# Four unused tensors that move the stationary matmul buffers by some bytes within a partition

## What is computed

```python
def first_block(x, p, ...):
    h = x
    for i in range(2):                      # i = 0: gated linear attention; i = 1: differential attention
        h = h + mixer(rms_norm(h, norm_mix[i]))
        h = h + swiglu(rms_norm(h, norm_ffn[i]), ffn_w_in[i], ffn_w_out[i])   # D_FF = 2816
        gate = sigmoid(rms_norm(h, ple_norm[i]) @ ple_w_gate[i])
        h = h + gate * (p[i] @ ple_w_proj[i])                                # p[i]: 256 wide
    return h

def second_block(x, ...):
    h = x
    for i in range(2):                      # i = 0: short convolution; i = 1: block attention, 16 heads
        h = h + mixer_2(rms_norm_2(h, norm_g[i]))
    return h
```

## Time and profile before

| | |
|---|---|
| median of the runs (lowest, highest) | 986.59 us (985.86, 987.36) |
| span of the profiled execution, first to last instruction | 983.4 us |
| median less span | 3.2 us |
| TensorE busy | 956.9 us, 97% |
| TensorE weight loads | 773.6 us, 79% |
| VectorE / ScalarE / GpSimd busy | 609.7 / 510.3 / 74.0 us |
| TensorE in the chain that ended last | 87% |
| line 1304 in that chain | 76% |
| granted clock of TensorE, mean | 0.996 |

### The profile page before, as it was taken

One profiled execution on the slowest core, in us unless ns is written; L12 is line 12 of the kernel. 1 busy time (PEld: TensorE's weight loads), 2 busy tenths in 40 slices (PEclk: granted clock), 3 DMA queues, 4 the chain that ended last, 5 costly groups with the idle time before them and its releaser, 6 DMA issues.

```text
span 983.4 us, 13238 instructions
## 1 busy us (share of the span) xinstructions
PE 956.9 (97%) x4532; PEld 773.6 (79%) x4532; DVE 609.7 (62%) x895; ACT 510.3 (52%) x821; POOL 74.0 (8%) x82
## 2 busy tenths in 40 slices
PE   7999999999999999878999999999999999999998
PEld 6786688888888888656788888888878888878777
DVE  5774556665655477886575565644577776565552
ACT  6854355434444466567563444443754444666470
POOL 0000000000000005531100000000000000302000
PEclk9999999999999999999999999999999999999999
DMA  7643246556555456332366555544555554542411
GB/s 280 215 154 118 96 144 200 189 173 193 190 193 176 146 166 209 119 105 74 98 214 191 186 178 189 175 172 161 203 181 186 189 195 146 192 152 96 145 60 43
DMA packets 45629, 159.73 MB, mean 162 GB/s; under 512 B 5099, under 2 KB 6891, under 8 KB 45580
## 3 DMA queue, kind: packets, MB, share of 16 engines
q1 hardware_dynamic: 45580, 159.06, 49.1%
HBM read 157.99 MB, written 1.05 MB: 162 GB/s over the span
## 4 chain that ended last, share of the span: by engine, by line
PE 87%; DVE 7%; ACT 2%; POOL 2%; issue 1%; DMA 1%; POOLq 0%; SPq 0%; ACTq 0%; DVEq 0%
PE bank L1304 76%; PE bank L1326 2%; DVE wlo L767 1%; PE bank L1528 1%; PE bank L1456 1%; DVE df_stat L1087 1%; PE bank L1479 1%; PE bank L1628 1%; PE bank L1710 1%; PE bank L1709 1%; ACT df_p L629 1%; PE bank L1732 1%; DVE df_m L1060 1%; DMA h<-x_dram 1%; PE bank L1718 0%
## 5 line engine op out<-in xcount | busy, mean ns | idle before, releaser
L767 DVE TENSOR_TENSOR wlo<-raw,whi 128x1024 fp32r<-128x1024 f32 (+1 forms) x297 | 350.6, 1217 | 66.3 <-ACT whi L418 66.1
L418 ACT ACTIVATE whi<-raw 128x1024 fp32r<-128x1024 f32 (+1 forms) x297 | 306.0, 1057 | 143.4 <-PE bank L1304 115.0
L1304 PE MATMUL bank<-whi,x_hi 128*128 128x512 f32 x592 | 236.9, 400 | 0.4 <-DVE x_lo L783 0.4
L1304 PE MATMUL bank<-whi,x_lo 128*128 128x512 f32 x592 | 231.2, 390 | 0.0
L1304 PE MATMUL bank<-wlo,x_hi 128*128 128x512 f32 x592 | 230.7, 390 | 0.0
L1304 PE MATMUL bank<-whi,y_hi 128*128 128x512 f32 x400 | 160.5, 401 | 0.8 <-DVE y_lo L1185 0.4
L1304 PE MATMUL bank<-whi,y_lo 128*128 128x512 f32 x400 | 157.0, 393 | 0.0
L1304 PE MATMUL bank<-wlo,y_hi 128*128 128x512 f32 x400 | 156.8, 392 | 0.0
L1304 PEld LDWEIGHTS bank<-whi,x_hi 128*128 128x128 f32 x592 | 111.2, 188 | 29.9 <-issue 7.1
L1304 PEld LDWEIGHTS bank<-whi,x_lo 128*128 128x128 f32 x592 | 111.1, 188 | 23.9
L1304 PEld LDWEIGHTS bank<-wlo,x_hi 128*128 128x128 f32 x592 | 111.3, 188 | 21.2
(11 more groups left out here) (208 smaller groups left out, 933.3 us busy)
## 6 DMA issues: line engine op xcount, KB each, us to landing
raw<-stream_dram SPq DMA_DIRECT2D x296, 512.0 KB, 4.2
h<-x_dram SPq DMA_DIRECT2D x4, 256.0 KB, 3.4
out<-h SPq DMA_DIRECT2D x4, 256.0 KB, 2.0
consts<-consts_dram SPq DMA_DIRECT2D x1, 576.0 KB, 8.9
p_tok<-p_dram SPq DMA_DIRECT2D x1, 512.0 KB, 9.4
rows<-rows_dram SPq DMA_DIRECT2D x1, 256.0 KB, 9.6
gla_wgate<-wgate_dram SPq DMA_DIRECT2D x1, 132.0 KB
raw<-stream_dram SPq DMA_DIRECT2D x1, 128.0 KB, 2.6
```

The lines of the kernel that those rows point to most:

```text
L418: A(whi[:, u % RING, 0:w], raw[:, u % RAW, 0:w], ACT.Copy).then_inc(sem("w_hi"), 1)
L767: V.tensor_tensor(wlo[:, u % RING, 0:w], raw[:, u % RAW, 0:w], whi[:, u % RING, 0:w].bitcast(F32), ALU.subtract).then_inc(sem("w_lo"), 1)
L1304: last = T.matmul(bank[pair + t][:, :], lhs[a][:, kt, t * P:(t + 1) * P], w[:, u % RING, kk * NW:(kk + 1) * NW], start=part != 1 and k == ...
```

## The change

Four tensors that no instruction reads or writes are declared between the others. That is the whole change.

```diff
         h = sb("h", [P, TT, D])
+        sb("before_x", [P, 16])
         X = (sb("x_hi", [P, KT, SEQ], F32R), sb("x_lo", [P, KT, SEQ], F32R))
+        sb("before_y", [P, 48])
         Y = (sb("y_hi", [P, KT, SEQ], F32R), sb("y_lo", [P, KT, SEQ], F32R))
+        sb("before_p", [P, 72])
         PT = (sb("p_hi", [P, 2, SEQ], F32R), sb("p_lo", [P, 2, SEQ], F32R))
         p_tok = sb("p_tok", [P, 2, TT, PLE])
         cols = sb("cols", [P, N_COLS])
@@
         neg_half = sb("neg_half", [P, 16])
         rstd_q = sb("rstd_q", [P, TT])
+        sb("before_phases", [P, 48])
         ident = consts[:, K_ID:K_ID + P]
```

## The result

The changed kernel took 992.28 us in the median of 13 runs (988.66 to 994.71), the kernel before 986.59 (981.37 to 991.46, 13 runs). The ratio is 1.0046, with a 95% interval of 1.003 to 1.0063. The change makes the kernel slower, by some 4.5 to 7 us. The forecast was 983.7 us, faster. The measured time lies in the stated range, which was drawn to hold every case of a loss too, but the change has the other sign.

The account below looks back on a forecast made before the run. TensorE, busy 97% of the span, was taken as the bound. Span 983.4 - 3.2 (`mid`) + 0.3 (`PT`) + 0 = 980.5 us, plus 3.2 gives 983.7 us; range of 8 in 10: 978 to 1002 us.

Parts of the forecast that it names:

- the term of `X`, 128 to 192: 1776 matmuls with `X` stationary: taken as 0, with 10.1 us more as the bound if they took `mid`'s pace.
- 416 is slow since it is no multiple of 64: Reading of the two phases seen: 416 is 6 x 64 + 32 and slow; 192 and 384, multiples of 64, cost 0.
- The argument that 64 bytes of the stream last about one step: 64 of the moving 2048 bytes take 7.1 ns, the step is 6.4 ns; phase 416 touches 9 pieces, 128 covers 8.
- `mid` gained 3.2 us: 528 matmuls with `mid`, phase 416 to 128: forecast 3.2 us less, FFN-out's piece of 96 at 21.8 us from 22.40.
- `Y` at 384: 1200 matmuls with `Y`, phase 128 to 384: taken as 0, with 6.8 us more as the bound.
- `PT`: 48 matmuls with `PT`, phase 128 to 160: forecast 0.3 us more, at `mid`'s slow pace.
- Transposes and plain matmuls: 480 transposes and some 470 mixer matmuls: taken as 0, bounds 3.1 us more and some 3.0 us less.
- the lost lock: Rival: pace needs both streams at matching phases; `X` alone 993.8 us, `Y` alone 990.5; chance 0.26, 0.14 for one buffer.
- the slow restart behind transposes at phase 128: Trace row cited for a rival: behind transposes ten steps of 232 ns each, then eight of 226 ns, at phase 128 too.
- Its full form, both buffers: Rival case where `X` and `Y` both lose the pace and `mid` gains: 14.0 us more, 1000.6 us, chance 0.12.
- The 3.2 us that the prediction put around the span: Step from span to time: the median stands 3.2 us above the profiled span, so 980.5 us becomes 983.7 us.
- The rule of the Trainium skill: TensorE's operands use independent ports and lines of 16 bytes: no phase should matter, time stays 986.6 us.

Follow-up runs that it names:

- e9: The kernel before with `X` alone moved, to phase 192; `Y` and `PT` stay at 128, `mid` at 416: 995.61 us, ratio 1.0098.
- e3: The kernel before with the moving rings and `X` at phase 192, `Y` at 384, `PT` at 448, `mid` at 256: 990.08 us in one run.
- e8: The kernel before with everything from `raw` on 64 bytes up and `mid` at 192, so rings and all four stationary buffers at phase 192: 983.84 us, ratio 0.9979.
- e10: The kernel before with `X`, `Y`, `PT` and `mid` at phase 192 and the moving rings left at 128: 1001.71 us, ratio 1.0154.
- e11: The kernel before with the moving rings alone at phase 192; `h` and all four stationary buffers stand at 128: 985.39 us in one run.
- e2: The kernel before with one pad of 56 words ahead of the scratch region, `mid` going from phase 416 to 128: 984.12 us, ratio 0.9975.
- e1: The changed kernel with the pad ahead of `X` removed and 16 words added ahead of `Y`, so `X` is back at 128: 984.18 us, ratio 0.9978.
- e6: The kernel before with rings at 128 and small offsets: `X` at 144, `Y` at 368, `PT` at 136, `mid` at 132: 989.93 us in one run.

## Why the prediction was wrong

**The step that failed** is the term of `X`, 128 to 192, for which the prediction took 0. It was 8.8 us (e9), near the upper bound of 10.1. The reading behind it was that 416 is slow since it is no multiple of 64. Two phases had been seen, and one property in which they differ was picked. In the kernel before, the rings stood at 128 as well, so equal phases and a good phase could not be told apart from its trace. e3, e8, e10 and e11 tell them apart: it is the distance to the moving ring. What `X` met is a distance of 64, at which a matmul takes 233.3 ns where it took 227.6, in 1776 matmuls.

The argument that 64 bytes of the stream last about one step proved nothing. In the count of the prediction, a slice of `mid` at a distance of 4 bytes touches nine pieces of 64 bytes, as at 32, and has nearly the same pace, but `X` at 64 touches only eight, as at 128, and is slow as well.

**What was right.** `mid` gained 3.2 us, 1.6 in each layer, and its piece went to 21.81 us where 21.8 was named. `Y` at 384 moved by next to nothing (0.08 us in the 528 matmuls of FFN-in), but for another reason than given: its distance is 256. That this term was right is luck. `PT` costs 0.07 us in each of its four products, 0.3 us, as taken. Transposes and plain matmuls cost nothing that can be seen: the mean of L1628, now L1632, is 277 ns in both kernels. In e2 the scratch buffers moved by 224 bytes and the identity kept its phase, and every stretch but FFN-out is within 0.13 us of the kernel before, the start and the two with falls of the clock set aside. In e1, where the identity moved to phase 32, the stretches without `PT` are within 0.07, the same three set aside.

**The rival that came true** is the lost lock, with `X` alone: 993.8 us forecast, 992.28 measured. It had a chance of 0.14 together with `Y` alone. Its sign in the trace was the slow restart behind transposes at phase 128, and that row deserved more weight than a count of two phases. The price was some 1.3 us high, since the mixer stages absorb part. Its full form, both buffers, was 1000.6 us with the gain of `mid`. e10 has both lost and no gain of `mid`, which makes 1003.8 us by the same sum, and took 1001.71.

**A smaller slip.** The 3.2 us that the prediction put around the span are 1.8: the profiled run after has a span of 990.5 and a time of 992.28. The rest of the 3.2 was the spread by the clock between the profiled run and the median.

**The rule of the Trainium skill** named in the prediction ("SBUF — State Buffer", sections "SBUF: two separate sides" and "Who interferes with whom": independent ports for TensorE's two operands, and TensorE waits for nobody) would have every pace alike. e10 and e8 differ by 17.9 us with the stationary buffers at the same phases, and e11, where the stationary buffers have the phases of e2 and the two moving rings alone have another, has 229.0 ns with `X`, `Y` and `mid` in place of the 227.3 to 228.1 of e2. So here the measurement decides against what that rule would give. What in the chip makes the difference is not shown. The 216 ns that the prediction takes for a floor from the Trainium skill, "TensorE: Matmul & The Clock Gate", section "Back-to-back issue gap", stand there as the gap of an isolated matmul. No stretch here came to it: the least means are near 226.7 ns.

**What stays open.** Why equal phases modulo 256 are fast, why 192 costs 2 ns in a steady stretch and 224 costs 6 to 7, and what sets the rhythm where one distance has two paces (e6). That the pace goes by the distance and not by one buffer's phase is shown for multiples of 64; the other distances stand in one buffer of one run each, but for 32. No distance gave steady stretches faster than those at distance 0, near 226.7 ns; distances between those of the table were not tried.

**A version that beats both kernels** is e2: one pad of 56 words ahead of the scratch region, so that the rings and all four stationary buffers have phase 128, ratio 0.9975. e8 and e1 are not told apart from it.

## What to carry to other kernels

Where a dense stream of matmuls like this one bounds the kernel (fp32r, 512 columns, a weight load for each), try the same start address modulo 256 for its moving and stationary buffers, and look at the addresses again after every change to the allocations: one small tensor in front can shift all behind it. Other types and widths were not measured here. Where a trace shows one instruction at two paces, list everything that is equal in the fast cases before choosing the cause; a property *between* two operands looks like a property of one as long as the other never moves. One run with four buffers at four phases answers as much as four runs, when each buffer's pace can be read by itself.

## What the hardware showed beyond expectation

- The start of the moving buffer relative to the stationary one changes the pace of 128 x 512 fp32r matmuls from 227 to up to 234 ns, while the recorded weight load has a median of 188 ns in the kernels before and after.
- One float32 value (4 bytes) of distance costs 5 ns a matmul (`mid` in e6, 232.5 ns against 227.2).
- Two moving buffers at different phases, 128 and 192, gave 234.5 ns with `X`, more than the distances 0 and 64 by themselves (227.9 and 233.3).
- The granted clock fell to 1.2 GHz for 3.4 or 6.8 us in only some executions of the same program, behind waits of 3.0 and 3.3 us and also, without any wait, at the eight matmuls of 33 rows. Much of the spread of this kernel goes with it.
